# A two-block network on one core: the eight blocks of a rounded weight chunk stand 258 columns apart instead of 256

## The reference, cut to what matters

```python
p = h @ w_in                               # 256x1024 @ 1024x6672, two layers
merged = sigmoid(gate_dn) * (o_dn @ w_branch_dn) + sigmoid(gate_hg) * (o_hg @ w_branch_hg)
x = x + merged @ w_out
gate, up = split(h @ w_up, (2816, 2816))   # 256x1024 @ 1024x5632, four layers in all
x = x + (silu(conv(gate) + bias) * up) @ w_down
```

## Time and profile before

| | |
|---|---|
| median of three runs | 1676.87 us (1676.51 to 1679.12) |
| profiled execution: span from first to last instruction | 1673.4 us |
| profiled execution: its own whole time | not listed apart from its span; the runs' median is 3.5 us above the span |
| TensorE busy (matmul / weight load) | 1625.0 us (97%) / 1549.8 us (93%) |
| VectorE busy | 1218.8 us (73%) |
| ScalarE busy | 989.4 us (59%) |
| data moved | 246.04 MB, mean 147 GB/s |
| mean granted TensorE clock | 0.994 |

### The profile page before, as it was taken

One profiled execution on the slowest core, in us unless ns is written; L12 is line 12 of the kernel. 1 busy time (PEld: TensorE's weight loads), 2 busy tenths in 40 slices (PEclk: granted clock), 3 DMA queues, 4 the chain that ended last, 5 costly groups with the idle time before them and its releaser, 6 DMA issues.

```text
span 1673.4 us, 29412 instructions
## 1 busy us (share of the span) xinstructions
PE 1625.0 (97%) x12534; PEld 1549.8 (93%) x12534; DVE 1218.8 (73%) x1715; ACT 989.4 (59%) x1494; POOL 7.9 (0%) x14
## 2 busy tenths in 40 slices
PE   8999899999999999899999999999999999899998
PEld 7999899999989999899999988878999988799997
DVE  7889736777758789646777657766688758678864
ACT  7775555556546784565566542356677645567753
POOL 0000000000000000000000000000000000000000
PEclk9999999999999999999999999999999999999999
DMA  7422125455554412126555552620455544055551
GB/s 272 171 77 77 51 77 201 160 195 200 178 200 151 151 54 77 51 76 227 179 194 182 186 187 104 228 75 2 167 186 179 200 176 158 1 202 189 189 191 62
DMA packets 35843, 246.04 MB, mean 147 GB/s; under 512 B 4096, under 2 KB 4480, under 8 KB 6656
## 3 DMA queue, kind: packets, MB, share of 16 engines
q1 hardware_dynamic: 35712, 244.15, 41.1%
HBM read 243.09 MB, written 1.05 MB: 146 GB/s over the span
## 4 chain that ended last, share of the span: by engine, by line
PE 81%; DVE 11%; ACT 5%; issue 1%; DMA 1%; SPq 0%; DVEq 0%; ACTq 0%
PE PS L402 81%; DVE SB L1753 2%; DVE SB L1762 2%; DVE WL L1753 2%; ACT SB L1111 2%; DVE SA L1753 2%; ACT WH L1114 1%; DVE SB L2006 1%; DVE SB L2010 1%; PE PS L405 1%; DMA RAW<-w_in 0%; DVE SA L1920 0%; ACT SB L1691 0%; DVE SA L1762 0%; ACT SA L1111 0%
## 5 line engine op out<-in xcount | busy, mean ns | idle before, releaser
L402 PE MATMUL PS<-XH,WH 128*128 128x256 f32 (+1 forms) x2536 | 714.5, 282 | 10.8 <-DVE WL L1753 6.7
L402 PE MATMUL PS<-XL,WH 128*128 128x256 f32 (+1 forms) x2536 | 712.9, 281 | 0.0
L402 PE MATMUL PS<-XH,WL 128*128 128x256 f32 (+1 forms) x2536 | 712.5, 281 | 0.0
L1114 ACT CAST WH<-RAW 128x2048 fp32r<-128x2048 f32 (+1 forms) x229 | 427.0, 1865 | 399.1 <-PE PS L402 364.1
L1753 DVE TENSOR_TENSOR WL<-RAW,WH 128x2048 fp32r<-128x2048 f32 (+1 forms) x229 | 511.5, 2234 | 124.4 <-ACT WH L1114 120.3
L402 PEld LDWEIGHTS PS<-XH,WH 128*128 128x128 f32 (+1 forms) x2536 | 477.1, 188 | 15.6 <-issue 6.0
L402 PEld LDWEIGHTS PS<-XL,WH 128*128 128x128 f32 (+1 forms) x2536 | 475.2, 187 | 2.7 <-issue 1.9
L402 PEld LDWEIGHTS PS<-XH,WL 128*128 128x128 f32 (+1 forms) x2536 | 474.9, 187 | 0.3
L402 PE MATMUL PS<-INHL,WH 128*128 128x512 f32 (+1 forms) x1216 | 334.7, 344 | 1.2 <-DVE INHL L1753 1.2
L402 PE MATMUL PS<-INHL,WL 128*128 128x256 f32 x960 | 270.0, 281 | 0.0
L402 PEld LDWEIGHTS PS<-INHL,WH 128*128 128x128 f32 x1216 | 210.3, 188 | 29.2 <-ACT INHL L1114 1.5
(11 more groups left out here) (142 smaller groups left out, 1456.7 us busy)
## 6 DMA issues: line engine op xcount, KB each, us to landing
RAW<-w_in SPq DMA_DIRECT2D x51, 1024.0 KB, 4.8
RAW<-w_up SPq DMA_DIRECT2D x44, 1024.0 KB, 4.7
RAW<-f_in SPq DMA_DIRECT2D x44, 1024.0 KB, 4.7
RAW<-w_down SPq DMA_DIRECT2D x22, 1024.0 KB, 4.8
RAW<-f_out SPq DMA_DIRECT2D x22, 1024.0 KB, 4.7
RAW<-a_w_in SPq DMA_DIRECT2D x10, 1024.0 KB, 4.7
RAW<-w_out SPq DMA_DIRECT2D x8, 1024.0 KB, 4.9
RAW<-w_bdn SPq DMA_DIRECT2D x4, 1024.0 KB, 4.9
```

The lines of the kernel that those rows point to most:

```text
L402: return e.matmul(out, l, r, start=start, stop=stop, skip_group_check=True)
L1114: e.copy(out, x).then_inc(*A.up(*key, of=of))
```

## The change

The slots of WH and WL grow from 2048 to 8 x 258 = 2064 columns, and block k begins at column 258 k of its slot instead of 256 k (1032 bytes apart instead of 1024). Chunks of fewer than 2048 columns stay contiguous. The rounding copy and the subtraction now write, and the subtraction reads, a pattern of eight rows of 256 with a step of 258; the raw side stays contiguous and is only viewed in the same shape. The matmuls find their operand through `cut_of`, or by the block's number. Their number, order, shapes and waits stay. To make room, the unused tile MZ leaves the constants: C shrinks by 128 columns, and its transfer with it. What lies behind WH moves by 192 bytes a partition, what lies behind WL by 384, and what lies behind C by -128.

```diff
+WSTEP = 258
+WSLOT = 8 * WSTEP
 CN = {n: i * 128 for i, n in enumerate(
-    ["ident", "TU", "TL", "MF", "MZ", "MB", "MP", "ROT"])}
+    ["ident", "TU", "TL", "MF", "MB", "MP", "ROT"])}
...
-        WH, WL = sb("WH", NWS * 2048, R), sb("WL", NWS * 2048, R)
+        WH, WL = sb("WH", NWS * WSLOT, R), sb("WL", NWS * WSLOT, R)
...
         def half(W, i):
-            s = (nth[i] % NWS) * 2048
-            return W[:, s:s + plan[i][1]]
+            s = (nth[i] % NWS) * WSLOT
+            if plan[i][1] < 2048:
+                return W[:, s:s + plan[i][1]]
+            return v3(W[:, s:s + WSLOT], 8)[:, :, 0:256]
+        def cut_of(W, at_, n=128):
+            return W[:, at_ // 256, at_ % 256:at_ % 256 + n]
+        def whole(x):
+            return v3(x, 8) if x.shape[1] == 2048 else x
...
-                            mm(o, wh[:, s], xh[:, x], k == 0 and j == 0, False)
-                            mm(o, wh[:, s], xl[:, x], False, False)
-                            last = mm(o, wl[:, s], xh[:, x], False, k == nk - 1)
+                            mm(o, cut_of(wh, s), xh[:, x], k == 0 and j == 0, False)
+                            mm(o, cut_of(wh, s), xl[:, x], False, False)
+                            last = mm(o, cut_of(wl, s), xh[:, x], False, k == nk - 1)
...
-                        pairs.append((XH[:, x], XL[:, x], wh[:, s], wl[:, s]))
+                        pairs.append((XH[:, x], XL[:, x], wh[:, k], wl[:, k]))
...
-                        mm(v3(p[:, :], 2), wh[:, ws], INboth[:, :, xs], k == 0, False)
-                        last = mm(p[:, 0:256], wl[:, ws], INH[:, xs], False, k == 21)
+                        mm(v3(p[:, :], 2), cut_of(wh, ws), INboth[:, :, xs], k == 0, False)
+                        last = mm(p[:, 0:256], cut_of(wl, ws), INH[:, xs], False, k == 21)
...
-                    cp(half(WH, i), raw(i), "w hi", i)
+                    cp(half(WH, i), whole(raw(i)), "w hi", i)
...
-                    low(half(WL, i), raw(i), half(WH, i), "w lo", i)
+                    low(half(WL, i), whole(raw(i)), half(WH, i), "w lo", i)
...
-    put("MZ", 0.0)
```

More of the change, by code:

```diff
@@ L33 @@
 CN = {n: i * 128 for i, n in enumerate(
-    ["ident", "TU", "TL", "MF", "MZ", "MB", "MP", "ROT"])}
-CN_COS, CN_SIN = 8 * 128, 8 * 128 + 256
-CN_CC, CN_CS = 8 * 128 + 512, 8 * 128 + 527
-CN_CM, CN_CV = 8 * 128 + 542, 8 * 128 + 542 + 32
+    ["ident", "TU", "TL", "MF", "MB", "MP", "ROT"])}
+CN_COS, CN_SIN = 7 * 128, 7 * 128 + 256
+CN_CC, CN_CS = 7 * 128 + 512, 7 * 128 + 527
+CN_CM, CN_CV = 7 * 128 + 542, 7 * 128 + 542 + 32
 CN_W = CN_CV + 32
@@ L439, in feat @@
                         for j in range(2):
-                            s = slice(k * width + (g + j) * 128, k * width + (g + j) * 128 + 128)
+                            s = k * width + (g + j) * 128
                             o = p[:, j * 256:j * 256 + 256]
-                            mm(o, wh[:, s], xh[:, x], k == 0 and j == 0, False)
-                            mm(o, wh[:, s], xl[:, x], False, False)
-                            last = mm(o, wl[:, s], xh[:, x], False, k == nk - 1)
+                            mm(o, cut_of(wh, s), xh[:, x], k == 0 and j == 0, False)
+                            mm(o, cut_of(wh, s), xl[:, x], False, False)
+                            last = mm(o, cut_of(wl, s), xh[:, x], False, k == nk - 1)
                     last.then_inc(*P.up("ps", *key, g // 2))
@@ L463, in tokm @@
                     for k in range(8):
-                        s, x = slice(k * 256, k * 256 + 256), slice(k * 256 + j * 128, k * 256 + j * 128 + 128)
-                        pairs.append((XH[:, x], XL[:, x], wh[:, s], wl[:, s]))
+                        x = slice(k * 256 + j * 128, k * 256 + j * 128 + 128)
+                        pairs.append((XH[:, x], XL[:, x], wh[:, k], wl[:, k]))
                     last = tri(p[:, j * 256:j * 256 + 256], pairs, st)
@@ L788, in down @@
                         p = ps[key] if k else bank(*key)
-                        xs, ws = slice(k * 256, k * 256 + 256), slice(u * 512 + f * 128, u * 512 + f * 128 + 128)
+                        xs, ws = slice(k * 256, k * 256 + 256), u * 512 + f * 128
                         w.wait_ge(*A["in hi", st, k // 2])
                         w.wait_ge(*V["in lo", st, k // 2])
-                        mm(v3(p[:, :], 2), wh[:, ws], INboth[:, :, xs], k == 0, False)
-                        last = mm(p[:, 0:256], wl[:, ws], INH[:, xs], False, k == 21)
+                        mm(v3(p[:, :], 2), cut_of(wh, ws), INboth[:, :, xs], k == 0, False)
+                        last = mm(p[:, 0:256], cut_of(wl, ws), INH[:, xs], False, k == 21)
                         if k == 21:
@@ L1727, in scalar @@
                 w.wait_ge(*s_first[n]["raw"])
-                cp(half(WH, 0)[:, s], raw(0)[:, s], "w hi first", n)
+                cp(half(WH, 0)[:, 2 * n:2 * n + 2], v3(raw(0)[:, s], 2), "w hi first", n)
                 if n == 3:
@@ L2597, in vector @@
                 w.wait_ge(*A["w hi first", n])
-                low(half(WL, 0)[:, s], raw(0)[:, s], half(WH, 0)[:, s], "w lo first", n)
+                s = slice(2 * n, 2 * n + 2)
+                low(half(WL, 0)[:, s], whole(raw(0))[:, s], half(WH, 0)[:, s], "w lo first", n)
                 if n == 3:
```

## The result

The changed kernel takes 1681.71 us (1679.78 to 1685.00, 7 runs) against 1676.38 us for the kernel before (1673.20 to 1679.12, 7 runs): a ratio of 1.0039 with a 95% interval of 1.0030 to 1.0049. It is slower by 5.3 us. The profiled execution has a span of 1678.8 us, 5.4 more than before, at a granted clock of 0.996 (0.994 before).

A forecast was written before the change was run, and what follows sets the result against it. TensorE, busy 97% of 1673.4 us, was taken as the bound. Terms 0 + 0 + 0.1 - 0.2 + 0 = -0.1 us, with 3.5 us from span to median, gave 1676.8 us, range 1672 to 1683; no change had 0.76.

The forecast's parts named there:

- the smaller losses: Rival: copy or subtraction pays for its rows where VectorE is the path, 5.8 us, giving 1682.6 us; chance 0.04.
- Part 5 of the sum: Addresses: everything behind WH moves by multiples of 64 bytes and no instruction changes; taken as 0.
- Part 1: Weight loads from shifted blocks in TensorE's matmuls: a start off the round address costs nothing; taken as 0.
- the 6 ns of cover: TensorE: a weight load taken as 112 ns beside a matmul pace of 117.9, so loads may slow 5% for nothing.
- 16 us is the most that can be won: Weight loads: 16-column loads ran only 2.1 ns a matmul faster, over 7536 matmuls, so placement could win no more.
- the slower rival: Shifted weight loads outlast their cover; 10% longer costs 33 us, giving 1710 us; sign: starts over 119 ns apart; chance 0.10.
- the faster one: Rival: the round step cost TensorE something; pace falls towards 115.8 ns, time by up to 16 us to 1661; chance 0.10.
- Parts 2 and 3: Moving blocks in tokm, at most 0.3 us, taken as 0; eight-row rounding copy and subtraction, taken as +0.1 us.
- Part 4: Constants at the start: 64 KB of 815 KB no longer sent, 0.24 us at 272 GB/s; taken as -0.2 us.

The follow-up runs named there:

- the chosen distances: The kernel before without MZ, with four gaps putting WL 128 bytes and XH, XL and INHL 192 bytes from WH, modulo 256: 1649.92 us against 1675.05, ratio 0.9853.
- the grid: Bare matmuls without the network: feat's 48 for 512 settings of WL, XH, XL, mean 118.2 ns; the down projection's pair for 64 settings, mean 349.5 ns.
- the bare stream's random settings: Bare matmuls without the network: feat's 48 for 400 settings with WL, XH and XL at random multiples of 8 bytes against WH; mean 119.1 ns.

## Why the prediction was wrong

The forecast was "no change", 1676.8 us; the change makes the kernel slower by 0.39%, 1681.7 us. That this lies inside the range, and near the 1682.6 us of the smaller losses, is luck: those were to come from the copy and the subtraction, which pay nothing. No part of the sum and no rival had the mechanism that the runs show.

- *Part 5 of the sum failed*: "All that lies behind WH moves by multiples of 64 bytes. No instruction changes for it, and I take 0." Moving WL alone costs 0.65%, moving the activations alone 0.41%, and moving both by 256 bytes nothing. The changed kernel's bases with its longer slots, at the old step, cost 0.54%. This term was put at nothing with no row behind it.
- *Part 1 had the wrong reason and so the wrong zero.* I looked for the price of a weight load that begins off a round address. None shows: blocks at odd multiples of 8 bytes are no slower as weights (117.9 against 118.3 ns).'s 112 ns and the 6 ns of cover were not tested. What the step changes is the distance between the block being loaded and the operand moving past. With the bases at their old distances the step and its longer slots cost 0.31%. Step and bases together cost 0.39%, not the sum of the two. That the start matters less once the distance walks from block to block is a reading of this, and no run tests it.
- *The evidence against it was misread.* "The pace is also the same for a moving operand out of XH, XL or INHL, which lie at unrelated addresses" rested on means over a repeating group. Inside the group the intervals differ: 116.3 ns after XH,WH, 118.5 after XL,WH, 118.5 after XH,WL. The recorded durations in the earlier trace rows can't show that, only differences of starts can, and the earlier trace rows has them (881.17 - 881.05) with a resolution of 10 ns.
- *The bound on a gain was wrong.* "16 us is the most that can be won" took the 16-column loads of the earlier trace rows for a stream without interference. With the chosen distances that same chunk runs at 113.3 ns, from 116.1, and the gain is 25 us. Reading fewer weights did not take the effect away.
- *Neither rival named the cause.* Full-width starts stayed under 119 ns apart, so the slower rival's sign is missing. For the faster one, no run shows a price of the round step as such: it kept before at 117.8 ns and 346.8 ns, an arrangement slightly better than the grid's mean (118.2 and 349.5).
- Parts 2 and 3 held within their bounds. `tokm` pays 1.2 ns a matmul, 0.3 us in all, which is the bound that part 2 gave before it took 0. The copy and the subtraction pay nothing. Part 4, the constants' 64 KB, can't be told in the times (ratio 1.0003 without them, with an interval of 0.9994 to 1.0011). The traces hint at more than the 0.2 us of the forecast at the start: the chain's first run of 696 matmuls begins at 213.36 us before and between 211.1 and 212.3 us in the changed kernel and the eight experiments without MZ that keep a pace of about 118 ns. There is only one trace of the kernel before, and nothing of it is left in the whole time.
- The test that I named for the slower rival, with the 16-column chunk unchanged, was no test: it went from 116.1 to 116.8 ns though its own layout had not changed, while its distance to XH and XL had. With everything moved by 256 bytes it has 116.1 ns.
- The 3.5 us that the forecast added to the span compared different executions: in every run that lists both, the time is 1.8 us above the span. This moves the forecast and the time before alike.

The sum with the measured paces: 7420 x 0.62 ns = 4.6 us in `feat`, 704 x 3.2 = 2.3 us in the down projections, 768 x 1.4 = 1.1 us in the branch products and 0.3 us in `tokm`, 8.3 us. The span grew by 5.4. The other 3 us lie outside the four long pieces, which alone have 5.5. The changed kernel is 1.1 us ahead where the first piece begins, and the execution profiled before had two more stretches at half clock; how the 3 us divide was not followed, and in the mixers TensorE waits for other engines, and later matmuls there need not make the end later.

The runs show that a moving operand pays for a start off 16 bytes: 1.2 ns over the triple where XH, two thirds of it, is off, and 3.7 ns in `tokm` when every block is (there the distances moved by 8 bytes too). Weights show no such cost. The Trainium skill (Advanced Engine Details and Errata, section SBUF Cachelines) says that memory is read in lines of 16 bytes and that two hits on a line are enough to hide a change of line. A moving operand that starts in mid-line touches 65 lines instead of 64, with two hits or more on each, so by that rule it should cost nothing; if the one more line costs as much as the others, it is 118/64 = 1.8 ns, an estimate from that page and the pace. The boundary of 16 bytes agrees with the runs, the free change of line does not.

Open: what in the chip has the period of 256 bytes. The runs show that the addresses of the two TensorE operands against each other set the pace for the most part, that no other engine is needed, that it comes with data of all zeros, and that the rhythm has a memory. That the load and the moving read meet in the same part of the memory would fit, and no run shows it.

## What to carry to other kernels

When TensorE is the bound and its matmuls are short, read the differences of starts, sorted by operand, before believing that addresses don't matter; a tensor that grows or vanishes ahead of the operands changes them all, and a control with the same addresses modulo 256 bytes separates that from the edit itself. Such a distance can be chosen for nothing: a bare stream on the chip finds good arrangements, and a few unused columns between the tensors put one into the kernel. Time it there as well, since the kernel followed the stream for its best setting (113.6 against 114.0 ns) and not for every other. Keep the start of a moving operand on 16 bytes.

## What the runs showed of the hardware that was not expected

- Back-to-back fp32r matmuls of 128x128 by 256 columns start 113.8 to 120.4 ns apart, by the addresses of the two operands, now and of the group before, with a period of 256 bytes (352 groups of 16).
- In feat's order of three operand pairs the 512 settings on 32 byte steps run from 114.0 to 123.8 ns, 8% apart, with a mean of 118.2.
- A moving operand that starts at an odd multiple of 8 bytes takes longer: `tokm` at 121.1 ns against 117.4 with all blocks 8 bytes later, and 119.5 against 118.3 ns in the bare stream's random settings. The same start costs a weight load nothing (117.9 against 118.3).
- Patterns of eight rows cost ScalarE's cast and VectorE's subtraction nothing: 1906 and 2287 ns for 2048 columns, 1908 and 2287 in one row.
